# The forget gate's sums and keys of an hgrn stage are made in the tail of the rwkv stage before it

## What is computed

```python
def hgrn2_branch(p, lb, gn_g):
    q, f, i, g = _split(p, (B_WIDTH, B_WIDTH, B_WIDTH, B_WIDTH))
    log_f = jnp.logaddexp(jnp.log(lb), jnp.log1p(-lb) + jax.nn.log_sigmoid(f))
    k_in = (1.0 - lb) * jax.nn.sigmoid(-f)
    ...

def hgrn2_chunk_step(state, inp):
    q, k, g, v = inp
    b = jnp.cumsum(g, axis=2)
    diff = b[:, :, :, None, :] - b[:, :, None, :, :]
    decay = jnp.exp(jnp.where(causal[:, :, None], diff, -jnp.inf))
    scores = jnp.einsum('bhtd,bhsd,bhtsd->bhts', q, k, decay)
    ...
```

## Time and profile before

| | us |
|---|---|
| median of 3 runs | 2986.98 |
| lowest, highest | 2983.28, 2988.97 |
| time of the profiled execution | 2983.27 |
| span of the profiled execution | 2981.4 |
| PE busy in it | 2686.6 (90%) |
| DVE busy | 1861.0 (62%) |
| ACT busy | 1363.2 (46%) |
| mean granted TensorE clock | 0.938 |

### The profile page before, as it was taken

One profiled execution on the slowest core, in us unless ns is written; L12 is line 12 of the kernel. 1 busy time (PEld: TensorE's weight loads), 2 busy tenths in 40 slices (PEclk: granted clock), 3 DMA queues, 4 the chain that ended last, 5 costly groups with the idle time before them and its releaser, 6 DMA issues. The chain is left out here.

```text
span 2981.4 us, 58180 instructions
## 1 busy us (share of the span) xinstructions
PE 2686.6 (90%) x25276; PEld 2292.0 (77%) x25276; DVE 1861.0 (62%) x2628; ACT 1363.2 (46%) x1925; POOL 83.8 (3%) x120
## 2 busy tenths in 40 slices
PE   7887779999896689999998898899999988978999
PEld 6775658888775568888887775688888877746888
DVE  5765767966746767946556544676565655346764
ACT  5523246656414256645454232555454542326543
POOL 0010000000110000000001100000000011000000
PEclk9997989999987899999998897999999989889999
DMA  5311224554201134555532120345555421203453
GB/s 221 111 59 57 71 72 172 206 212 158 106 37 57 57 127 170 198 188 177 205 143 94 58 74 26 126 173 200 213 187 207 146 81 58 78 24 133 178 199 127
DMA packets 54686, 386.57 MB, mean 130 GB/s; under 512 B 6688, under 2 KB 7328, under 8 KB 8352
## 3 DMA queue, kind: packets, MB, share of 16 engines
q1 hardware_dynamic: 54432, 382.86, 35.9%
HBM read 381.79 MB, written 1.05 MB: 128 GB/s over the span
## 5 line engine op out<-in xcount | busy, mean ns | idle before, releaser
L336 PE MATMUL banks<-normed_high,weights_high 128*128 128x256 f16 (+1 forms) x4096 | 1141.3, 279 | 44.1 <-DVE weights_low L322 21.2
L337 PE MATMUL banks<-normed_low,weights_high 128*128 128x256 f16 (+1 forms) x4096 | 1140.3, 278 | 0.0
L338 PE MATMUL banks<-normed_high,weights_low 128*128 128x256 f16 (+1 forms) x4096 | 1139.2, 278 | 0.0
L322 DVE SCALAR_TENSOR_TENSOR weights_low<-weight_ring,weights_high 128x2048 f16<-128x2048 f32 x336 | 765.3, 2279 | 369.2 <-ACT weights_high L316 354.9
L316 ACT ACTIVATE weights_high<-weight_ring 128x2048 f16<-128x2048 f32 x306 | 580.6, 1898 | 222.6 <-PE banks L338 209.7
L336 PEld LDWEIGHTS banks<-normed_high,weights_high 128*128 128x128 f16 (+1 forms) x4096 | 409.4, 100 | 122.3 <-issue 29.8
L336 PE MATMUL banks<-projected,weights_high 128*128 128x256 f16 x1696 | 465.7, 275 | 29.3 <-DVE projected L347 29.3
L337 PE MATMUL banks<-projected,weights_high 128*128 128x256 f16 x1696 | 465.7, 275 | 0.0
L338 PE MATMUL banks<-projected,weights_low 128*128 128x256 f16 x1696 | 465.4, 274 | 0.0
L338 PEld LDWEIGHTS banks<-normed_high,weights_low 128*128 128x128 f16 (+1 forms) x4096 | 408.6, 100 | 55.5
L337 PEld LDWEIGHTS banks<-normed_low,weights_high 128*128 128x128 f16 (+1 forms) x4096 | 408.3, 100 | 55.3 <-issue 1.3
(11 more groups left out here) (399 smaller groups left out, 2943.4 us busy)
## 6 DMA issues: line engine op xcount, KB each, us to landing
weight_ring<-w SPq DMA_DIRECT2D x356, 1024.0 KB, 4.8
small_weights<-small SPq DMA_DIRECT2D x2, 1280.0 KB, 8.0
constants<-const SPq DMA_DIRECT2D x1, 1697.0 KB, 10.3
weight_ring<-w SPq DMA_DIRECT2D x2, 640.0 KB, 3.8
residual<-xt SPq DMA_DIRECT2D x1, 1024.0 KB, 4.7
small_weights<-small SPq DMA_DIRECT2D x2, 512.0 KB, 11.0
out<-residual SPq DMA_DIRECT2D x4, 256.0 KB, 2.3
parameters<-par SPq DMA_DIRECT2D x2, 115.5 KB, 9.8
```

Of the source, the lines that this page charges most:

```text
L322: nc.vector.scalar_tensor_tensor(out=self.part(self.mem.w_low, g), in0=self.part(self.mem.ring, g), scalar=W_SCALE, in1=self.part(self.mem ...
L336: pe.matmul(out, w_high, high, start=start, stop=False, skip_group_check=skip)
L337: pe.matmul(out, w_high, low, start=False, stop=False, skip_group_check=skip)
L338: return pe.matmul(out, w_low, high, start=False, stop=stop, skip_group_check=skip)
```

## The change

A class `HgrnDecay` holds the work that hgrn did ahead of its main loop: the bound's logits, |f| and max(f, -40) (`sizes`), the bound (`bound`), the combination of the logarithms and the four scans (`sums`), the scaled keys (`keys`) on DVE; the exponentials (`exps`), the logarithms and the sigmoid (`logs`) on ACT. `rwkv_stage` now runs them for n = 1: `sizes` before the copy of `rhs`, `bound` before the copy of `sa`, `sums` and `keys` before the copy of `y`; `exps` and `logs` between ACT's last solver copy and filler tile 6. `logs` ends with a square root of a constant. `cs`, `key` and the small values live in `small_weights`, `t1` and `t2` in two rwkv operands (`btp`, `ktp`). `hgrn_stage` opens with `exponents(0)` and low part 0; low part 1, the clearing and the copy of the values come after the factors of level 0, and ACT's second `high` after the exponential of level 0, its slots one level later than before.

```diff
@@ rwkv_stage, DVE
                 solver.vector(dve, nc, sig, n, link, say, beside[n])
+                if n:
+                    decay.sizes(link, say, need)
                 need("rhs_summed", n + 1)
                 say(V.tensor_copy(rhs.rearrange("p (b a) -> p b a", b=2), ps[:, 6:8, 0:T]), "rhs")
+                if n:
+                    decay.bound(link, say, need)
                 need("sa_summed", n + 1)
                 say(V.tensor_copy(sa, ps[:, 4, :]), "sa")
+                if n:
+                    decay.sums(link, say, need)
+                    decay.keys(link, say, need)
                 need("y_summed", n + 1)
@@ rwkv_stage, ACT
             solver.scalar(act, nc, sig, 1, {2: [lambda: norm.root(act, nc, say, 1)], 3: [high(5)]})
+            decay.exps(link, say, need)
+            decay.logs(link, say, need)
             out(6)
             high(6)()
@@ HgrnDecay, the ACT part
+    def exps(self, link, say, need):
+        A, lbt, t2 = self.nc.scalar.activation, self.lbt, flat(self.t2)
+        need("lb_logits", 1)
+        say(A(lbt[:, 1:3, :], lbt[:, 1:3, :], ACT.Exp), "lb_exp")
+        need("f_sizes", 1)
+        link(A(self.t1, self.t1, ACT.Exp, scale=-1.0))
+        link(A(t2, t2, ACT.Exp, scale=-1.0))
+        say(A(self.t1, self.t1, ACT.Ln, bias=1.0), "log_terms")
+
+    def logs(self, link, say, need):
+        A, t2 = self.nc.scalar.activation, self.t2
+        need("lower_bound", 1)
+        for h in range(MT_):
+            say(A(t2[:, h, :], t2[:, h, :], ACT.Ln, bias=1.0, scale=self.lb[:, h:h + 1]), "log_terms")
+        say(A(flat(self.key), flat(self.f), ACT.Sigmoid, scale=-1.0), "forget_inverse")
+        link(A(self.still, self.mem.c("ones", 1), ACT.Sqrt))
@@ hgrn_stage, DVE (the work ahead of the loop is gone)
             exponents(0)
+            gates.low(dve, nc, sig, 0)
             for n in range(len(ALL)):
@@
-                if n:
+                if n == 0:
+                    gates.low(dve, nc, sig, 1)
+                    say(V.memset(flat(acc), 0.0), "cleared")
+                    need("values_turned", 1)
+                    say(V.tensor_copy(vt, two(0)), "values_by_token")
+                else:
                     gather(n - 1)
@@ hgrn_stage, ACT (exps and logs are gone)
-            gates.high(act, nc, sig, 1)
-            gates.scalar(act, nc, sig, 0)
             for n in range(len(ALL)):
                 need("exponents", n + 1)
                 say(A(flat(diff[n % 2]), flat(diff[n % 2]), ACT.Exp), "decays")
-                gates.scalar(act, nc, sig, n + 1)
+                if n == 0:
+                    gates.high(act, nc, sig, 1)
+                gates.scalar(act, nc, sig, n)
+            gates.scalar(act, nc, sig, len(ALL))
             gates.scalar(act, nc, sig, len(ALL) + 1)
```

More of the change, by code:

```diff
@@ L1524, in rwkv_stage @@
     norm = TokenNorm(mem, sig, rhs, kh_t, rwkv.stat, HEADS, HD, GN_EPS)
+    decay = HgrnDecay(nc, mem, sig, btp, ktp)
     TURN_BANK = (7, 6)
@@ L1761, in hgrn_stage @@
     cut = Cutter(mem.beside_gates)
-    key, cs, acc, vt = (cut(NH, T) for _ in range(4))
+    decay = HgrnDecay(nc, mem, sig, mem.proj[:, 0:NH, :], mem.proj[:, NH:2 * NH, :])
+    key, cs = decay.key, decay.cs
+    acc, vt = (cut(NH, T) for _ in range(2))
     diff = [cut(NH, T) for _ in range(2)]
@@ L1766, in hgrn_stage @@
     t1, t2 = mem.proj[:, 0:NH, :], mem.proj[:, NH:2 * NH, :]
-    lb, lb_inv, lbt, stat = cut(NH), cut(NH), cut(3, NH), cut(2 * NBLK * NH)
+    stat = cut(2 * NBLK * NH)
     ps, par = mem.ps, mem.par
@@ L1794, in _ @@
             V = nc.vector
[L1796 to L1826, removed]
             def exponents(n):
```

40 lines of the change are left out of this document (added).

## The result

| | before | after |
|---|---|---|
| median, us | 2987.97 (4 runs) | 2945.34 (4 runs) |
| lowest, highest | 2983.28, 2992.43 | 2942.12, 2949.07 |
| time of the profiled execution | 2983.27 | 2948.04 |
| its span and mean granted clock | 2981.4, 0.938 | 2945.5, 0.944 |

The ratio is 0.9857, with a 95% interval of 0.9844 to 0.987: 42.6 us by the medians. The forecast was 2951 with a range of 2944 to 2964, so the time lies inside it, but the gain was forecast at 35.8 us and the interval of the measured one reaches from 39 to 47. The two profiled executions, on which the sum was made, differ by 35.2 us of time and 35.9 us of span. Which of the two sizes is the change's own was the main thing left to find out.

What follows compares the result with a forecast made beforehand. PE, 90% busy, was taken as the bound, waiting in hgrn's opening on a DVE-ACT chain. Openings save 17.8 and 18.0 us, the tail costs nothing: 2983.3 - 35.8 = 2947.5 profiled, 2951 median, range 2944 to 2964.

Steps and rivals of the forecast that it cites:

- the sum: Both hgrn openings: 17.8 us saved in the first layer and 18.0 in the second, 35.8 us in all.
- What bounds the kernel: PE, busy 90% of the span; in hgrn's opening it waits 4.1 and 14.2 us behind a DVE-ACT chain.
- where the programs meet again: End of hgrn's factors of level 3; before, 42.17 and 42.43 us after DVE's first instruction; same work follows.
- rival 3: Gain given back in hgrn's second half, waiting for gates or slabs; if half went, 2969 us; chance 5%.
- The opening, 24.4 us: hgrn's start: DVE's listed work reaches the end of the factors of level 3 after 24.4 us, DVE the bound.
- neither margin: hgrn's opening: ACT's exponential of level 2 was to be 2 us early, PE's scores of level 1 1.5 us.
- The gain, 35.8 us: Both hgrn openings shorten to 24.4 us, from 42.17 and 42.43, saving 35.8 us in all.
- The tail costs nothing: rwkv's tail: moved DVE and ACT work fits idle time, 2.4 us left before rhs's copy, 4.4 before y's.
- Rival 1, the cold opening: PE at 1.2 GHz through hgrn's opening, costing 7 us a layer, 14 in all: 2965 us median; chance 5%.
- Rival 2, a late chain: Moved chain late in rwkv's tail; beyond 4.4 us each microsecond costs one per layer; 10 us late: 2962; chance 3%.
- the 4.4 us that I counted: rwkv's tail: DVE's keys end at 244.9, the copy of y comes at 249.30, leaving a 4.4 us margin.

Runs made afterwards that it cites:

- tail_only: Changed rwkv stage in front of the hgrn stage of before, so the work is done twice: 2985.94 us against 2987.51 before, ratio 0.9992.
- warm_open: The changed kernel plus 28 unread matmuls on PE where it waits for low part 0: 2948.22 us, ratio 0.987 to the kernel before.
- pad12: The changed kernel plus twelve useless DVE additions (15.1 us) behind the scaled keys, ahead of the copy of y: 2975.92 us, ratio 0.9965 to before.
- pad5: The changed kernel plus five useless DVE additions (6.3 us) behind the scaled keys, ahead of the copy of y: 2954.48 us, ratio 0.989 to before.
- order_only: The kernel before with only the opening's new order, the work staying in hgrn: 2988.38 us, ratio 1.0002 to before.

## Why the prediction came out as it did

- *What bounds the kernel; where the programs meet again.* Right. Nothing was given back behind the factors of level 3, so rival 3 did not come; the rest of the stage even took 0.6 to 1.7 us less in each layer, at a higher clock, which the sum did not have.
- *The opening, 24.4 us.* It took 24.71 in both layers. The 0.3 us are small gaps: low part 0 started at 2.0 instead of 1.9, and 0.16 us went by ahead of the clearing. ACT's exponential of level 2 ended 14.7 us into the stage (forecast 14.5), slot 0 took 7.1 us (6.9), and neither margin was used up.
- *The gain, 35.8 us.* 35.2 by the openings. 2947.5 was forecast on the time of the profiled execution, and it was 2948.0; that it met to half a microsecond is luck, since outside the openings this profile was 5.2 us longer than that of before up to the first hgrn stage and 6.0 us shorter behind the first opening. Adding 3.7 us for the median comes to the same as taking the gain from the median of before, and the 2951.2 lies near the mean of all 13 runs, 2950.6. The single medians came out at 2945.3, 2953.7 and 2954.7: the clock of single executions moves them. That the recorded gain (42.6) was 7 us larger than the sum is for the most part this; 1.2 to 2.3 us are the rest of the stage.
- *The tail costs nothing.* Right, by `tail_only`, and each margin as worked out: 2.63 us left ahead of the copy of rhs (2.4), 4.37 ahead of the copy of y (4.4), the root wanted 12 us behind ACT's last tile (the profile shows 11.8).
- *Rival 1, the cold opening.* Did not come. In the change slot 0 began at the full clock, with five matmuls 0.11 us apart, fell to 0.51 from 276.7 to 280.1 us and was back at 0.99 behind it. `warm_open` shows that this cost nothing: with PE kept busy slot 0 ran at 1.00 instead of 0.76, and the opening was as long. The rule of the Trainium skill (TensorE: Matmul & The Clock Gate, Part 1), that activity has to lift the throttle, agrees with slot 0 at 0.76 after its wait and at 1.00 with PE kept busy.
- *Rival 2, a late chain.* The mechanism exists, as `pad12` shows, but my price for it was wrong at both ends. Cover was longer than the 4.4 us that I counted, since the filler tiles behind y cover more (`pad5`: 1.9 us late at no cost). Beyond the cover a microsecond of PE's waiting cost more than one in each layer (8.3 us cost about 11 in `pad12`), since the clock had fallen in the hole.

What I missed in the experiments' expectations was ACT's table load: in `order_only` it stood behind a wait, and DVE waited 1.1 us for the exponential behind it in each layer.

## What to carry to other kernels

A chain of small DVE and ACT steps that opens a stage can be had for nothing in the tail of the stage before, if PE is busy there and those engines wait for it; look for the wait that PE has at the end of the chain, but price the gain at the next point where the engines meet: `order_only` took 4.5 us off PE's 14.2 us wait in each layer and gained 3 us at the most over both. Cover is not the one wait that the profile names: follow the delayed engine to the next wait for PE, and where PE is the bound, count a hole that does reach it at more than its length. Where another engine is the bound, as DVE in this opening, PE's half clock costs nothing. And where single executions of the same program differ by 12 to 16 us, size a change by stretches between fixed instructions, not by two medians of four.

## What the runs showed of the hardware

TensorE's granted clock differs from one execution to the next at the same instructions with nothing changed ahead of them: the same 24 matmuls took 4.89 us in one and 8.19 in another (1.00 against 0.66 over the window from 80 to 90 us). The time of the whole kernel goes with it (2981.3 us at a mean of 0.938, 2988.7 at 0.934). After PE stood still for 7.1 us its clock was 0.50 for the next 6 us, and two tiles there took 7.8 us instead of 5.4. A table load of ACT takes 1.28 us. Where it ran ahead of a wait (at 283.19 us of before, then 5.50 us of waiting) it was hidden; where it ran behind one (in `order_only`, after 6.21 us of waiting) DVE had to wait 1.08 us for the exponential.
